# Sample rows of seven projection groups as plain fp32 matmuls in four column groups, with the weights' division moved ahead and five banks for the projections

## The chip, the cores and the metric

The kernel runs on 1 core of one Trainium2 chip. The metric is the device time of one execution in microseconds (us); less is better.

## What is computed

One inference step of a one-layer hybrid decoder. 1024 prompt rows (`SEQ`) and 8 sample rows (`DEC_BATCH`, one new token each) of width 1024 are normalised and go through one combined input projection, whose columns are split among an attention head group with three branches and a retention head group:

```python
parts = jnp.split(rms_norm(x, norm_g) @ w_in, SPLIT_POINTS, axis=-1)
q = rms_norm(parts[0].reshape(b, t, NSA_HEADS, HEAD_DIM), q_norm_g)
...
q_r = rotary(parts[9].reshape(b, t, RET_HEADS, RET_KDIM), pos)
k_r = rotary(parts[10].reshape(b, t, RET_HEADS, RET_KDIM), pos) * (RET_KDIM ** -0.5)
v_r = parts[11].reshape(b, t, RET_HEADS, RET_VDIM)
```

`project` is called for the prompt and for the sample with the same weights `w_in`. Behind it come compression of keys and values, attention, retention with a state, and one output projection with a residual.

## The kernel before, in words

The program is a row of stages, each with its own block of five engine programs and a barrier between them (`between`). The change lies in the first, `project` (line 186).

**Tiles and groups.** The 1032 rows are nine row tiles: eight of 128 prompt rows (`t` = 0 to 7) and the sample tile of 8 rows (`t` = `TT` = 8, `NT` = 9). The columns are eight groups in the order `qr, kr, vr, zr, q, wg, kv, zn`, all of 512 columns but `wg` (280). The loops run over groups outside and row tiles inside; `i = 9g + t`. The depth of 1024 is eight tiles of 128 (`KT`).

**Split precision.** Rows and weights are each held as a rounded high part and a low part that is the rest. On TensorE `proj` (line 806) makes three matmuls per depth tile (lines 818 to 820: high by high, low weights by high rows, high weights by low rows), 24 for a row tile, the sample tile included. ScalarE's `split_w` (line 435, activation at 441) rounds a depth tile of the next group's weights to `w_high`; VectorE's `split_w` (line 586, subtraction at 590) makes `w_low`. The text calls each of these instructions a half; there are eight on either engine per group. There is one buffer of each part, so ScalarE waits per depth tile for `w_used`, which TensorE raises during the sample tile, the last user of a group's weights. The raw weights come over SP's queue (`load_w`, line 262), for each depth tile once the low part of the group before is made.

**Banks.** Row tile `i` accumulates in PSUM bank `i % 3`; `bank_free` (line 232), raised by VectorE, tells TensorE that the tile that used the bank last is evacuated. Banks 3 and 4 take transposes, 5 to 7 the retention's scores and outputs.

**Evacuation.** `evac` on ScalarE (line 447) and VectorE (line 593) turns the sums into rotated rows (`qr`, `kr`; the last addition on GpSimd, line 399), gated rows (`zr`, `zn`), or normalised rows (`q`, `wg`, `kv`: a square on ScalarE, sum and mean on VectorE at lines 640 and 642, the root on GpSimd at 384, the product on VectorE). `post` on TensorE (line 880) turns normalised rows by transposes, and ScalarE and VectorE split them (lines 497 and 682). In TensorE's loop (line 945) the `post` of tile `i - 1` stands behind the projection of tile `i`, that of the sample tile too.

**Retention inside vr.** TensorE's `turn_ret` (line 832), `score`, `grow` and `out_ret` work on one chunk of 128 rows per row tile, between parts of the projection. The turn of the first chunk waits until GpSimd has added all rotated rows of `qr` and `kr`, the sample rows among them.

**Order.** Each engine's program is written out by hand and runs in order; semaphores tie them.

## Time and profile before

| | |
|---|---|
| median of 3 runs | 1019.42 us (1018.35 to 1020.18) |
| the profiled execution's own time | 1015.06 us |
| its span in the profile | 1013.4 us |
| granted TensorE clock, mean | 0.968 of 2.4 GHz |
| TensorE (PE) busy | 933.8 us, 92% |
| VectorE (DVE) busy | 501.9 us, 50% |
| ScalarE (ACT) busy | 309.7 us, 31% |
| GpSimd (POOL) busy | 189.4 us, 19% |
| projection stage on TensorE, first to last projection matmul | 17 to 497 us |

Rows of a timeline give the start and the length in us, then engine, line, operation and operands (output first), how many instructions were merged into the row, and in brackets the idle time before it with what ended it. A matmul's recorded length is modelled and overlaps the next one, so the pace is read from the starts. A plain fp32 matmul (no split) is recorded as two passes, that is two rows or a count of two.

### The profile page before, as it was taken

The numbers are of one execution on the slowest core, as the hardware profiler recorded it, in microseconds if no ns is written. First come the engines' busy times: TensorE is split into PE (matmuls) and PEld (weight loads), VectorE is DVE, ScalarE is ACT, GpSimd is POOL, SyncE is SP. The second block draws the span as 40 slices with busy tenths as digits, with TensorE's granted clock in tenths as the row PEclk, the third lists the DMA queues.
The fourth block names the chain that finished last, engine by engine and source line by source line (L and its number), as shares of the span: only waits on it lengthen the run. The fifth ranks groups of instructions, "written<-read, shape, count | busy, mean of one in ns | idle before, by whom it ended". The sixth has DMA issues, their size and how long they took to land. (4 is left out here: it accounts for less than half of the span.)

```text
span 1013.4 us, 15464 instructions
## 1 busy us (share of the span) xinstructions
PE 933.8 (92%) x5223; PEld 706.3 (70%) x5223; DVE 501.9 (50%) x1072; ACT 309.7 (31%) x692; POOL 189.4 (19%) x234
## 2 busy tenths in 40 slices
PE   5999999999999989999778898999999996789998
PEld 3676879997768787868568775566665654566785
DVE  4764244446144555450156356766675744464522
ACT  4311032223032324241010355645655642211100
POOL 1222213333002221100053102111011021452000
PEclk9999999999999999999989778999999997999999
DMA  7407520002520023113395410000000025778621
GB/s 256 143 6 177 138 84 1 2 1 73 213 94 6 1 83 104 53 38 107 91 205 144 115 31 22 22 21 22 1 22 22 1 81 187 204 218 276 200 85 46
DMA packets 91004, 91.11 MB, mean 90 GB/s; under 512 B 27629, under 2 KB 69661, under 8 KB 90565
## 3 DMA queue, kind: packets, MB, share of 16 engines
q1 hardware_dynamic: 70546, 71.66, 23.4%
q10 hardware_dynamic: 16700, 9.36, 3.5%
q0 software_dynamic: 3680, 9.10, 3.2%
q8 instruction: 42, 0.69, 0.3%
q14 instruction: 36, 0.29, 0.1%
HBM read 75.51 MB, written 23.49 MB: 98 GB/s over the span
## 5 line engine op out<-in xcount | busy, mean ns | idle before, releaser
L818 PE MATMUL ps<-w_high,x_high 128*128 128x512 f32 (+3 forms) x576 | 225.3, 391 | 4.6 <-DVE w_low L590 2.7
L820 PE MATMUL ps<-w_high,x_low 128*128 128x512 f32 (+3 forms) x576 | 220.6, 383 | 0.0
L819 PE MATMUL ps<-w_low,x_high 128*128 128x512 f32 (+3 forms) x576 | 220.3, 382 | 0.0
L818 PEld LDWEIGHTS ps<-w_high,x_high 128*128 128x128 f32 (+1 forms) x576 | 102.9, 179 | 37.2 <-issue 7.4
L820 PEld LDWEIGHTS ps<-w_high,x_low 128*128 128x128 f32 (+1 forms) x576 | 102.6, 178 | 28.0
L819 PEld LDWEIGHTS ps<-w_low,x_high 128*128 128x128 f32 (+1 forms) x576 | 102.9, 179 | 26.1
L1629 PE MATMUL ps<-k_high,q_stack 128*128 128x512 f32 (+3 forms) x192 | 77.9, 409 | 12.8 <-DVE a_stats L1514 12.5
L384 POOL TENSOR_TENSOR stats<-stats,small 128x8 f32<-128x8 f32 (+3 forms) x35 | 40.8, 1165 | 226.1 <-DVE stats L642 170.8
L1629 PEld LDWEIGHTS ps<-k_high,q_stack 128*128 128x128 f32 x192 | 38.8, 202 | 54.4 <-DVE a_stats L1514 28.6
L1671 PE MATMUL ps<-weights_turned,v_nat 128*64 128x512 f32 x264 | 72.5, 631 | 0.0
L1630 PE MATMUL ps<-k_low,q_stack 128*128 128x512 f32 (+3 forms) x192 | 67.0, 356 | 0.0
L2246 PE MATMUL ps<-w_out_high,y_high 128*128 128x512 f32 (+1 forms) x144 | 61.1, 424 | 4.1 <-DVE w_out_low L1982 3.5
L1180 DVE COPY kcs<-ps 128x512 f32<-128x512 f32 x28 | 30.3, 1084 | 69.2 <-PE ps L1240 69.1
L1423 POOL TENSOR_TENSOR y_tile<-y_tile,branch_out 128x512 f32<-128x512 f32 x15 | 19.2, 1277 | 224.4 <-DVEq L1572 224.4
L2248 PE MATMUL ps<-w_out_high,y_low 128*128 128x512 f32 (+1 forms) x144 | 57.4, 399 | 0.0
L2247 PE MATMUL ps<-w_out_low,y_high 128*128 128x512 f32 (+1 forms) x144 | 57.2, 398 | 0.0
L1514 DVE CUSTOM_DVE_ANT_1 window_logits<-ps,bias_full 128x640 f32<-128x640 f32 (+3 forms) x56 | 39.1, 708 | 34.0 <-PE ps L1630 33.7
L1542 DVE COPY weights_turned<-ps 128x512 f32<-128x512 f32 x66 | 45.5, 690 | 20.3 <-PE ps L1650 15.8
L1444 ACT ACTIVATE full_logits<-full_logits,a_stats 128x128 f32<-128x128 f32 (+7 forms) x64 | 49.3, 771 | 20.3 <-DVE a_stats L1514 20.0
L441 ACT ACTIVATE w_high<-w_raw 128x512 fp32r<-128x512 f32 (+1 forms) x64 | 36.5, 602 | 57.2 <-PE ps L820 55.6
L1514 DVE CUSTOM_DVE_ANT_1 full_logits<-ps,bias_full 128x256 f32<-128x256 f32 (+6 forms) x56 | 45.0, 821 | 17.8 <-PE ps L1630 16.5
L1453 ACT ACTIVATE weights_turned<-ps 128x512 f32<-128x512 f32 x66 | 39.0, 591 | 47.9 <-PE ps L1650 47.9
(311 smaller groups left out, 1526.6 us busy)
## 6 DMA issues: line engine op xcount, KB each, us to landing
w_raw<-in_w_in SPq DMA_DIRECT2D x48, 256.0 KB, 4.4
tmp_skew<-tmp_table SPq DMA_DIRECT2D x8, 576.0 KB
bias_full<-tmp_skew SPq DMA_DIRECT2D x8, 512.0 KB, 5.4
w_out_raw<-in_w_out SPq DMA_DIRECT2D x16, 256.0 KB, 5.0
y_rows_in<-tmp_y SPq DMA_DIRECT2D x8, 512.0 KB, 4.5
x_rows<-in_x_prompt SPq DMA_DIRECT2D x8, 512.0 KB, 5.6
out_y_prompt<-out_rows SPq DMA_DIRECT2D x8, 512.0 KB, 5.5
x_tile<-in_x_prompt SPq DMA_DIRECT2D x6, 512.0 KB, 3.8
```

What stands on the lines that cost most here:

```text
L818: nc.tensor.matmul(out, s.xh[:, k, rows], s.wh[:, k, 0:w], start=(k == 0), stop=False)
L819: nc.tensor.matmul(out, s.xh[:, k, rows], s.wl[:, k, 0:w], start=False, stop=False)
L820: ins = nc.tensor.matmul(out, s.xl[:, k, rows], s.wh[:, k, 0:w], start=False, stop=(k == KT - 1))
L1444: nc.scalar.activation(lg[:, h, 0:P * n], lg[:, h, 0:P * n], ACT.Exp, scale=-1.0, bias=st[:, S_MIN + H * j + h:S_MIN + H * j + h + 1], acc ...
L1514: nc.vector.tensor_tensor_reduce(out=columns(lg[:, h, 0:1]), in0=columns(pair[:, 0:1]), in1=view(full[:, TT - n, h, 0:1], [H * P, n], [1, ...
L1542: nc.vector.tensor_copy(pt[:, k % RP, 1, :], bank(k, 1)).then_inc(taken_v, 1)
L1629: nc.tensor.matmul(out, q(h), s.kh[:, j, h // G, k0 + c:k0 + c + w], start=True, stop=False)
L1630: last = nc.tensor.matmul(out, q(h), s.kl[:, j, h // G, k0 + c:k0 + c + w], start=False, stop=not (masked and c == 0))
L1671: last = nc.tensor.matmul(s.ps[at, 6, :], s.v[:, j, t + 1 - n + b, at], pt[:, k % RP, kv, :], start=(b == 0), stop=(b == n - 1))
L2246: nc.tensor.matmul(to, yh[:, t % 2, k, 0:n], wh[:, k, cols], start=(k == 0), stop=False)
L2247: nc.tensor.matmul(to, yh[:, t % 2, k, 0:n], wl[:, k, cols], start=False, stop=False)
L2248: last = nc.tensor.matmul(to, yl[:, t % 2, k, 0:n], wh[:, k, cols], start=False, stop=(k == KT - 1))
```

## The change

Group `qr` is computed as before, its sample tile included. In the other seven groups the sample tile's 24 split matmuls are replaced:

- The 8 sample rows are kept in plain fp32, turned so that depth lies on partitions (`x_sample_turned`, copied by VectorE from the banks of the transposes).
- `sample_rows(g)` multiplies them with the raw weights of group `g`: eight plain fp32 matmuls, four depth tiles into four column groups of bank 5 (partitions 0, 32, 64, 96), in two rounds. It stands one group ahead: behind tile 4 of group `g - 1`, behind tile 7 in `qr`, and at the end of `vr`.
- `keep_parts(g)` on ScalarE copies the bank, four partial sums of 8 rows, to SBUF. At the sample tile's place one plain fp32 matmul with `to_rows`, a matrix of ones and zeros, adds the four parts into an ordinary bank (the fold); evacuation then goes on as before.
- `w_used` is raised in tile 7 (`last_tile`). ScalarE's `split_w` for the next group stands ahead of tile 7's evacuation; VectorE's eight halves are spread: four ahead of tile 7's evacuation and four ahead of the sample tile's in `kr` and `zr`; in `q`, `wg` and `kv` two inside tile 6's evacuation (between mean and root), three ahead of and two inside tile 7's, one ahead of the sample tile's. In `qr` and `vr` all eight stand where they stood.
- The projections may use banks 6 and 7 too, in all groups but `qr`, `vr` and the first three tiles of `zr`: the bank used longest ago is taken.
- The `post` of a group's tile 7 and of its sample tile move on TensorE into the next group: behind its tile 0, and behind four depth tiles of its tile 1. In `vr`'s first tile the turn stands behind seven depth tiles in place of five.
- SP waits for the sample rows of group `g - 1` before it loads the weights of group `g`.

The core of the diff:

```diff
+    bank_of, uses = [], []
+    for i in range(n_idx):
+        allowed = (0, 1, 2) if i < NT or 2 * NT <= i < 3 * NT + 3 else (0, 1, 2, 6, 7)
+        last_use = {b: max((j for j, c in enumerate(bank_of) if c == b), default=-1) for b in allowed}
+        bank_of.append(min(allowed, key=lambda b: (last_use[b], b)))
...
             def load_w(g):
+                if g >= 2:
+                    sp.wait_ge(parted, g - 1)
...
+            def keep_parts(g):
+                w = GROUPS[g][2]
+                act.wait_ge(parted, g)
+                act.wait_ge(projected, g * NT)
...
+                nc.scalar.activation(fold(g)[:, 0:w], s.ps[:, PART_BANK, 0:w], ACT.Copy).then_inc(parts_kept, 1)
...
+                    beside = g > 0 and KIND[g] != "vr"
+                    if t == (TT - 1 if beside else TT) and g + 1 < NG:
+                        split_w(g + 1)
                     if t == TT and g + 1 < NG:
-                        split_w(g + 1)
+                        keep_parts(g + 1)
...
+                    if meanwhile:
+                        split_w(i // NT + 1, meanwhile)
                     dve.wait_ge(k_root, ni + 1)
...
+                    beside, chain = g > 0 and KIND[g] != "vr", KIND[g] in ("wg", "kv", "q")
+                    if t == TT - 1 and beside and g + 1 < NG:
+                        split_w(g + 1, range(2, 5) if chain else range(0, 4))
                     if t == TT and g + 1 < NG:
-                        split_w(g + 1)
+                        split_w(g + 1, range((7 if chain else 4) if beside else 0, KT))
...
+                    if chain and g + 1 < NG and t in (TT - 2, TT - 1):
+                        evac(i, range(0, 2) if t == TT - 2 else range(5, 7))
+                    else:
+                        evac(i)
...
+            def sample_rows(g):
+
+                w = GROUPS[g][2]
+                if g >= 2:
+                    pe.wait_ge(parts_kept, g - 1)
+                else:
+                    pe.wait_ge(part_set, 1)
+                for r in range(2):
+                    for c in range(4):
+                        k = 4 * r + c
+                        pe.wait_ge(w_in[k], 16 * (g + 1))
+                        last = nc.tensor.matmul(s.ps[32 * c:32 * c + B, PART_BANK, 0:w], s.xrow[:, k, :], s.wraw[:, k, 0:w],
+                                                start=(r == 0), stop=(r == 1))
+                last.then_inc(parted, 1)
...
+                if g and t == TT:
+                    pe.wait_ge(parts_kept, g)
+                    nc.tensor.matmul(out, s.to_rows[:], fold(g)[:, 0:w], start=True, stop=True).then_inc(projected, 1)
+                    return
...
-                    if t == TT and k < KT - 1:
+                    if t == last_tile and k < KT - 1:
                         ins.then_inc(w_used, 1)
...
-                        proj(i, range(0, 5))
+                        proj(i, range(0, 7))
                         turn_ret(t)
-                        proj(i, range(5, KT))
+                        proj(i, range(7, KT))
...
+                elif t == 1 and post_evac_kind(i - 2):
+                    proj(i, range(0, 4))
+                    post(i - 2)
+                    proj(i, range(4, KT))
                 else:
                     proj(i)
-                if i >= 1 and post_evac_kind(i - 1):
-                    post(i - 1)
+                if t == (TT if kind == "vr" else 7 if i < NT else 4) and i // NT + 1 < NG:
+                    sample_rows(i // NT + 1)
+                due_now = i - 2 if t == 0 else i - 1
+                if i >= 2 and t < TT and post_evac_kind(due_now):
+                    post(due_now)
```

How the order moves, at three places. First VectorE at the end of group `q`, from the product of tile 6 to that of the sample tile (`q_doubled` is the product, `q_stack` the low parts of the tile before, `w_low` the division for `wg`). Before:

```order
L649 TENSOR_TENSOR q_doubled<-ps,stats 128x1024
L707 SCALAR_TENSOR_TENSOR q_stack<-ps,gain,q_stack 64x4x128 x2
L640 TENSOR_REDUCE stats<-squares 128x8
L642 TENSOR_SCALAR stats<-stats 128x8
L649 TENSOR_TENSOR q_doubled<-ps,stats 128x1024
L707 SCALAR_TENSOR_TENSOR q_stack<-ps,gain,q_stack 64x4x128 x2
L590 TENSOR_TENSOR w_low<-w_raw,w_high 128x280 x8
L640 TENSOR_REDUCE stats<-squares 8x8
L642 TENSOR_SCALAR stats<-stats 8x8
L654 TENSOR_TENSOR q_doubled<-ps,stats 8x4x64 x2
```

Now, from the two halves ahead of that same product:

```order
L618 TENSOR_TENSOR w_low<-w_raw,w_high 128x280 x2
L679 TENSOR_TENSOR q_doubled<-ps,stats 128x1024
L737 SCALAR_TENSOR_TENSOR q_stack<-ps,gain,q_stack 64x4x128 x2
L618 TENSOR_TENSOR w_low<-w_raw,w_high 128x280 x3
L668 TENSOR_REDUCE stats<-squares 128x8
L670 TENSOR_SCALAR stats<-stats 128x8
L618 TENSOR_TENSOR w_low<-w_raw,w_high 128x280 x2
L679 TENSOR_TENSOR q_doubled<-ps,stats 128x1024
L737 SCALAR_TENSOR_TENSOR q_stack<-ps,gain,q_stack 64x4x128 x2
L618 TENSOR_TENSOR w_low<-w_raw,w_high 128x280
L668 TENSOR_REDUCE stats<-squares 8x8
L670 TENSOR_SCALAR stats<-stats 8x8
```

The one run of eight halves has become four pieces of two, three, two and one between the steps of tiles 6 and 7.

Second TensorE at the same end, from the `post` of tile 6 to that of the sample tile (`8x512` are the sample tile's matmuls, `128x280` those of `wg`). Before:

```order
L890 MATMUL ps<-ident,q_doubled 128x128 x8
L818 MATMUL ps<-w_high,x_high 8x512
L819 MATMUL ps<-w_low,x_high 8x512
...
L820 MATMUL ps<-w_high,x_low 8x512
L890 MATMUL ps<-ident,q_doubled 128x128 x8
L818 MATMUL ps<-w_high,x_high 128x280
...
L820 MATMUL ps<-w_high,x_low 128x280
L916 MATMUL ps<-ident,q_doubled 128x8 x4
```

Now:

```order
L962 MATMUL ps<-ident,q_doubled 128x128 x8
L879 MATMUL ps<-row_parts_late,to_rows 8x512
L887 MATMUL ps<-w_high,x_high 128x280
...
L889 MATMUL ps<-w_high,x_low 128x280
L962 MATMUL ps<-ident,q_doubled 128x128 x8
L887 MATMUL ps<-w_high,x_high 128x280
...
L889 MATMUL ps<-w_high,x_low 128x280
L988 MATMUL ps<-ident,q_doubled 128x8 x4
```

The 24 matmuls have become one, tile 7's turn has moved behind the first tile of `wg`, and the sample tile's turn from there into its second tile.

Third TensorE in the first tile of `vr`, from the turn of the first chunk to its scores (`kt_zeroed`). Before:

```order
L841 MATMUL ps<-ident,q_ret 128x128 x4
L841 MATMUL ps<-ident,k_ret 128x128 x4
L818 MATMUL ps<-w_high,x_high 128x512
L819 MATMUL ps<-w_low,x_high 128x512
...
L852 MATMUL ps<-qt,kt_zeroed 128x128 x8
```

Now:

```order
L910 MATMUL ps<-ident,q_ret 128x128 x4
L910 MATMUL ps<-ident,k_ret 128x128 x4
L887 MATMUL ps<-w_high,x_high 128x512
L888 MATMUL ps<-w_low,x_high 128x512
L889 MATMUL ps<-w_high,x_low 128x512
L924 MATMUL ps<-qt,kt_zeroed 128x128 x8
```

Between turn and scores stand now three projection matmuls where nine stood.

## Rows read from the trace of the kernel before

**Rows 1.** The page's busy time of TensorE, its share and instructions.

```profile
PE 933.8 (92%) x5223; PEld 706.3 (70%) x5223; DVE 501.9 (50%) x1072; ACT 309.7 (31%) x692; POOL 189.4 (19%) x234
```

**Rows 2.** Stretches: us; PE, PEld, DVE, ACT, POOL busy (count), clock, DMA, GB/s.

```profile
129.81:145.75 15.94, 15.03 (x81) 9.94 (x80) 10.58 (x17) 7.32 (x12) 3.60 (x3) 1.00 0.27 89
233.78:244.26 10.48, 10.18 (x65) 6.53 (x64) 9.23 (x14) 5.87 (x11) 4.65 (x3) 1.00 0.01 3
290.59:296.62 6.03, 5.73 (x26) 2.08 (x24) 4.92 (x8) 5.08 (x9) 0.00 (x0) 1.00 0.12 45
347.59:366.35 18.76, 15.07 (x89) 11.18 (x88) 10.85 (x25) 7.51 (x19) 3.96 (x3) 0.91 0.33 113
...
387.26:390.47 3.21, 3.21 (x27) 2.09 (x25) 1.76 (x7) 3.14 (x10) 0.70 (x1) 1.00 0.13 40
387.26:397.97 10.71, 9.68 (x55) 6.85 (x53) 7.92 (x20) 6.06 (x18) 1.38 (x2) 1.00 0.09 26
439.95:452.45 12.50, 12.20 (x59) 7.17 (x57) 9.18 (x24) 10.29 (x22) 1.39 (x2) 1.00 0.08 24
```

**Rows 3.** Waits of PE, 80 to 500 us: waited for, us, times, longest.

```profile
PE ps L916 <- DVE q_stack L707: 3.4, 1, 3.4
PE ps L818 <- DVEq L629: 1.5, 1, 1.5
PE ps L896 <- DVE k_low L698: 0.7, 1, 0.7
```

**Rows 4.** Timeline of PE around a 32-column fp32 matmul block, 903 us.

```profile
903.19 0.40 PE L2247 MATMUL ps<-w_out_low,y_high 128*128 128x512 f32 x1
903.42 0.40 PE L2248 MATMUL ps<-w_out_high,y_low 128*128 128x512 f32 x1
903.75 2.77 PE L2215 MATMUL ps<-keys_turned,q_by_row 128*32 128x512 f32 x12
906.45 0.50 PE L2246 MATMUL ps<-w_out_high,y_high 128*128 128x512 f32 x1
```

**Rows 5.** Timeline of PE, 8-column fp32 matmuls in four column groups, 974 us.

```profile
973.97 0.28 PE L2278 MATMUL ps<-values_in_raw,pt_selected 128*8 128x128 f32 x2
973.99 0.28 PE L2278 MATMUL ps<-values_in_state,pt_selected 128*8 128x128 f32 x2
...
976.60 0.40 PE L2280 MATMUL ps<-cv_sample,pt_compressed 128*8 128x128 f32 x8
```

**Rows 6.** Timeline of PE around one table matmul in group qr, 41 us.

```profile
40.53 1.04 PE L929 MATMUL ps<-ident,x_tile 128*128 128x128 f32 x8
41.50 1.02 PE L937 MATMUL ps<-one_hot,rel_bias_masked 33*8 33x512 f32 x2
42.45 0.50 PE L818 MATMUL ps<-w_high,x_high 128*128 128x512 f32 x1
```

**Rows 7.** Timeline of DVE at the end of group q.

```profile
343.72 1.23 DVE L649 TENSOR_TENSOR q_doubled<-ps,stats 128x1024 f32<-128x1024 f32 x1 [1.75 <-POOL stats L384]
345.19 1.43 DVE L707 SCALAR_TENSOR_TENSOR q_stack<-ps,gain,q_stack 64x512 fp32r<-64x512 f32 x2 [0.24 <-DVE q_doubled L649]
347.62 0.69 DVE L640 TENSOR_REDUCE stats<-squares 128x8 f32<-128x512 f32 x1 [1.00 <-ACT squares L492]
...
353.19 2.97 DVE L590 TENSOR_TENSOR w_low<-w_raw,w_high 128x280 fp32r<-128x280 f32 x8
```

**Rows 8.** Timelines of ACT and DVE: eight halves of 512 columns, for kv.

```profile
388.31 4.28 ACT L441 ACTIVATE w_high<-w_raw 128x512 fp32r<-128x512 f32 x8
...
390.50 4.90 DVE L590 TENSOR_TENSOR w_low<-w_raw,w_high 128x512 fp32r<-128x512 f32 x8
```

**Rows 9.** Timelines of POOL and ACT in the first tile of vr.

```profile
138.84 1.27 POOL L399 TENSOR_TENSOR k_ret<-rotated 8x512 f32<-8x512 f32 x1 [6.10 <-DVE rotated L605]
...
141.78 1.20 ACT L570 ACTIVATE kt_zeroed<-ps 64x512 f32<-64x512 f32 x2
```

**Rows 10.** DMA issues of the page: KB each, us to landing.

```profile
w_raw<-in_w_in SPq DMA_DIRECT2D x48, 256.0 KB, 4.4
```

More of the change, by code:

```diff
@@ L167, in layout @@
     s.stat = m.put("stats", [P, 64])
+    s.xrow = m.put("x_sample_turned", [P, KT, B])
+    s.to_rows = m.put("to_rows", [P, B])
     assert m.at <= SB_END, m.at
@@ L212, in project @@
     cen = m.put("centred", [P, 512])
+    folds = [m.put("row_parts_early", [P, 512]), Memory(nc, s.rq_region + 4 * H * T).put("row_parts_late", [P, 512])]
+    fold = lambda g: folds[g // 4]
+    PART_BANK = 5
     vr = Memory(nc, s.kct_region).put("v_ret", [P, 2, 512])
@@ L220, in project @@
     kind_of = lambda i: KIND[i // NT]
+    bank_of, uses = [], []
[3 more added lines that the diff above has]
+        bank_of.append(min(allowed, key=lambda b: (last_use[b], b)))
+        uses.append(bank_of[:-1].count(bank_of[-1]))
+    uses_up_to = lambda b, g: bank_of[0:NT * g].count(b)
     stored = [[0, 0]]
@@ L231, in project @@
         projected, rows_in, = sem("projected"), sem("ret_rows_out")
-        bank_free = [sem(f"bank_free{b}") for b in range(3)]
+        bank_free = {b: sem(f"bank_free{b}") for b in (0, 1, 2, 6, 7)}
+        part_set, parted, parts_kept, rows_turned = sem("row_part_bank_set"), sem("row_parts"), sem("row_parts_kept"), sem("x_rows_turned")
         st_stored = [sem(f"st_stored{b}") for b in range(2)]
@@ L448, in evac @@
                 kind, t = kind_of(i), i % NT
-                n, ps = rows_of(t), s.ps[0:rows_of(t), i % 3, :]
+                n, ps = rows_of(t), s.ps[0:rows_of(t), bank_of[i], :]
                 if kind == "vr":
@@ L530, in square @@
                                      accum_out=s.stat[0:n, t:t + 1]).then_inc(sum_ready, 1)
+            def keep_parts(g):
+                w = GROUPS[g][2]
+                act.wait_ge(parted, g)
+                act.wait_ge(projected, g * NT)
+                if g == 1:
+                    act.wait_ge(tab_stored, 16)
+                if g == 4:
+                    act.wait_ge(rows_in, 48)
+                nc.scalar.activation(fold(g)[:, 0:w], s.ps[:, PART_BANK, 0:w], ACT.Copy).then_inc(parts_kept, 1)
             def x_high(t):
@@ L591, in split_w, with evac @@
                                             ALU.subtract).then_inc(w_low, 1)
-            def evac(i):
+            def evac(i, meanwhile=None):
                 kind, t = kind_of(i), i % NT
-                n, ps = rows_of(t), s.ps[0:rows_of(t), i % 3, :]
-                free = bank_free[i % 3]
+                n, ps = rows_of(t), s.ps[0:rows_of(t), bank_of[i], :]
+                free = bank_free[bank_of[i]]
                 if kind in ("qr", "kr"):
@@ L732, in x_low @@
                                             ALU.subtract).then_inc(low_ready, 1)
+                    if t == TT:
+                        nc.vector.tensor_copy(s.xrow[:, 4 * half:4 * half + 4, :], view(s.ps[:, 3 + j % 3, 0:1], [P, 4], [1, n])).then_inc(rows_turned, 1)
+                if t == TT:
+                    dve.wait_ge(rows_turned, 3)
+                    nc.vector.memset(s.ps[:, PART_BANK, :], 0.0).then_inc(part_set, 1)
             def keep_table(j):
@@ L739, in _ @@
             nc.vector.memset(s.stat[:], 0.0).then_inc(stat_set, 1)
+            dve.wait_ge(ident_ready, 2)
+            nc.vector.tensor_reduce(s.to_rows[:], view(s.ident[:, 0:1], [1, B], [32, 4]), AX, ALU.add).then_inc(rows_turned, 1)
             dve.wait_ge(scale_in, 32)
@@ L797, in _ @@
                         retention_norm(nc, s, dve, own, cen, P, s.ps[:, 7, :], r_out, t, gn_done, t - 1, cen_ready, gn_sq, gn_mean)
-                    evac(i)
+                    if chain and g + 1 < NG and t in (TT - 2, TT - 1):
+                        evac(i, range(0, 2) if t == TT - 2 else range(5, 7))
+                    else:
+                        evac(i)
                     if i >= 1 and post_evac_kind(i - 1):
@@ L808, in proj @@
                 n, w = rows_of(t), GROUPS[g][2]
-                if i >= 3 and some[0] == 0:
-                    pe.wait_ge(bank_free[i % 3], (i - 3) // 3 + 1)
+                out = s.ps[0:n, bank_of[i], 0:w]
+                last_tile = TT if g == 0 else TT - 1
+                if some[0] == 0:
+                    if uses[i]:
+                        pe.wait_ge(bank_free[bank_of[i]], uses[i])
+                    if bank_of[i] >= 6 and g == 1:
+                        pe.wait_ge(tab_kept, N_HOT)
+                    if bank_of[i] >= 6 and kind_of(i) == "zr":
+                        pe.wait_ge(r_scd, 2 * TT)
+                        pe.wait_ge(cen_ready, TT)
+                if g and t == TT:
+                    pe.wait_ge(parts_kept, g)
+                    nc.tensor.matmul(out, s.to_rows[:], fold(g)[:, 0:w], start=True, stop=True).then_inc(projected, 1)
+                    return
                 if g == 0 and some[0] == 0:
@@ L816, in proj @@
                     rows = slice(P * t, P * t + n)
-                    out = s.ps[0:n, i % 3, 0:w]
                     nc.tensor.matmul(out, s.xh[:, k, rows], s.wh[:, k, 0:w], start=(k == 0), stop=False)
@@ L824, in proj @@
                     return
-                if t == TT:
+                if t == last_tile:
                     ins.then_inc(w_used, 1)
@@ L849, in score @@
                     pe.wait_ge(state_set, 4)
+                    pe.wait_ge(parts_kept, KIND.index("vr"))
+                    for b in (6, 7):
+                        pe.wait_ge(bank_free[b], uses_up_to(b, KIND.index("vr")))
                 for e in range(2):
```

## The prediction, made before the changed kernel ran

> **What bounds the kernel now.** I read the page's table of busy time first, then the stretches at the ends of the projection groups, then TensorE's waits, and last single rows of matmuls that resemble the new ones. TensorE is busy for 92% of the span [rows 1]; in the projection stage (17 to 497 us) it is the path, because the stretches at every group's end show it busy for nearly their whole length [rows 2]. So what the change takes off TensorE there comes off the time, unless a wait takes its place. The waits of that stage are few and short [rows 3], and each sits near a group's end, where the change works. The stages behind the projection begin after a barrier and keep their code; I take them as moved, not changed.
>
> The sum is made against the profiled execution, 1015.06 us (span 1013.4). The median of the runs shown is 1019.42, 0.43% above it; the gain in us is subtracted from the median.
>
> **Removed.** A split-precision matmul of 512 columns starts 0.23 us after the one before it, 903.19 to 903.42 [rows 4], so a tile of 24 takes 5.55 us, sample tile or not: at zr's end the sample tile and the drain behind it take 6.03 [rows 2], which leaves 0.48 for the drain (TensorE waits for its own last matmul through `w_used`). The drain stays; it only moves to the end of tile 7. In wg, with 280 columns, the tile takes 3.21 [rows 2]. Six times 5.55 and once 3.21 make **36.5 us removed**.
>
> **Added: the sample rows.** Eight plain fp32 matmuls, 8 columns of weights each, recorded as two passes apiece. Two kinds of rows show their price. The 32-column fp32 matmuls of L2215, 512 wide, go in pairs of two column groups: 12 records from 903.75 to 906.45 [rows 4], 0.45 us for each round of two records with the change back to full width in it, and an entry of 0.33 where 0.23 is usual, 0.10 more. The 8-column matmuls of L2278, 128 wide, go four at a time, in exactly the placement the change uses: 96 records in 24 rounds from 973.97 to 976.60, 0.11 us a round [rows 5], a quarter of the 512-wide round, as the widths are. Four rounds then cost 4 x 0.45 + 0.10 = 1.90 us at 512 columns and 1.1 at 280 (by the ratio of columns). No row shows four groups at 512 columns; the low bound is this, the high one is one group after another (a rival below). I take the low one: it is the nearest in both respects. 6 x 1.90 + 1.1 = **12.5 us added**. Their data wait for nothing: the weights of the next group land 4.4 us after their issue [rows 10], early in the group, and the sample rows come behind tile 4 (7 in the first group, the last place in vr).
>
> The row on the way back to full width bears on a rule of the Trainium skill. The matmul at 906.45 starts some 0.1 us later than a round would make it [rows 4]. The Trainium skill, TensorEngine Tiling (Array Packing), Key Properties, states that a change of tiling mode drains TensorE. Read strictly, as the whole modelled tail of a 0.40 us matmul behind its 0.23 pitch, each of the 14 excursions would cost about 0.15 us more, and the sum would be 2 us smaller; by the rows it is as above.
>
> **Added: the fold.** One plain fp32 matmul per group, 8 columns by 512. Its like is the table's matmul in the first group: from 41.50 to the next projection matmul at 42.45 is 0.95 us [rows 6]; with the entry of 0.10 it is 1.05, in wg 0.65. Six and one make **6.95 us added**. So TensorE's own work falls by 36.5 - 12.5 - 6.95 = 17.05 us.
>
> **The division loses its cover.** ScalarE's eight halves for 512 columns take 4.28 us and VectorE's 4.90 [rows 8]; before, they ran beside the sample tile. Now `w_used` counts tile 7, and the next group starts 0.48 + 1.05 us behind it. I followed each end:
> - *vr to zr* (10.48 [rows 2]): the division starts when tile 7 ends; fold, growth, output and sample rows take about 7.9 us, longer than the 4.9 of the division. No wait.
> - *zr to q*: half of VectorE's halves lie beside tile 7, the rest behind one evacuation; the fifth is due about 4.2 us behind tile 7 and ready at 3.4. No wait. Five banks also end the wait of 1.5 us for a bank here (L818 on the queue of L629 [rows 3]): ScalarE's results stand late, but five tiles can now wait for it. **-1.5.**
> - *kr to vr* (15.94): the sample row's sum on GpSimd starts 9.03 us behind tile 7 [rows 2, 9]; half of the 6 us of division leaves that path, so it ends near 9.03 - 3.0 + 1.27 = 7.3 us. TensorE, with seven depth tiles in place of five ahead of the turn, arrives at 6.35 and waits 1.0 us; ScalarE's three copies behind the turn end 2.9 us after its start (the last at 142.98, the turn right behind the sum's end at 140.11 [rows 9]), and only eight transposes (0.97 with what follows [rows 6]) and three matmuls lie there, so about 1.3 more. Before, that place lost 0.8. New stretch 12.85 against 15.94: 3.1 instead of the 4.5 of the tile less the fold. **+1.4.**
> - *q to wg* (18.76, clock 0.91 in it): VectorE sets the pace. From the end of tile 7's matmuls: ScalarE's square is late by 0.4 behind its halves, so the reduction starts at 1.3; reduce and scale 0.9, the root 1.75, the product 1.23 [rows 7] end at 5.1; the low parts of tile 6, 1.43 [rows 7], at 6.5; the last half (2.97 / 8 [rows 7]) at 6.9. TensorE wants it at 5.2: 1.7 of wait. Then the sample row's evacuation and tile 7's low parts end near 11.8, wanted at 9.9: 1.9. One more of 0.4. With 9.5 us of work that is 13.5 in place of 18.76, 5.2 gained against 4.5 counted. **-0.7**; L916's 3.4 [rows 3] comes back as two shorter waits.
> - *wg to kv* (10.71): the last half is ready 0.7 late, while L896's 0.7 [rows 3] goes with the later turn. **-0.2.**
> - *kv to zn* (12.50) and zn's end: the last half is ready 0.7 before it is wanted. Nothing.
>
> The halves put between mean and root on VectorE are covered by the root's 1.75 us there [rows 7]; without that cover they would cost the chains of q, wg and kv up to 0.75 each time. The copies of the parts on ScalarE (7 of 0.6), VectorE's copies and the clearing of the bank lie where these engines are idle; uncovered, they would be about 5 us. SP's new wait before a load is on sample rows of two groups earlier, long done; the stores queued behind it are not held.
>
> **Sum:** 17.05 + 1.5 - 1.4 + 0.7 + 0.2 = 18.05 us. 1019.42 - 18.05 = **1001.4 us**. The unknowns are the new waits (I count 7.0 us of them; between none, which adds 7, and twice as many, which takes 7) and the granted clock: the stretch q to wg ran at 0.91 [rows 2] because of one long wait, and two shorter ones may or may not lower it. With a few us for the clock of the stages behind, whose phase moves, the forecast's own range is 995 to 1009.
>
> **The rivals.**
> 1. *The four column groups overlap only in part.* For it: no row has four streams of 512 columns. Against: [rows 4, 5]. Two at a time doubles the rounds: 6 x 1.8 + 1.0 = 11.8 us back, 1013.2. The Trainium skill, TensorE: Matmul & The Clock Gate, Measured speedup vs the span model, gives three column tiles 2.38 times one, not three; by it a round would stretch by a quarter, 2.9 us back, 1004.3, though the 24 rounds of four in [rows 5] show no stretch. Chance 0.07, two thirds of it for that milder form.
> 2. *The groups run one after another.* This ends on the other side: sixteen passes of 0.43 where four were counted, 12 x 0.43 = 5.1 us more in six groups and 2.8 in wg: 33.5 back, **1035, slower**. It decides from the point where a round lasts 2.6 times its present length, since 11.2 us of rounds stand against 18. Against it: [rows 4, 5] show the opposite. Chance 0.03.
> 3. *Waits at the group ends take most of the gain.* VectorE's program is in strict order, and a half that waits for ScalarE holds the evacuation behind it; if the last half came 1.5 us later than I count at all seven ends, 10 us go back: 1011. For it: q, wg and kv are chains in which every link was within 0.4 us of TensorE. Chance 0.12.
> 4. *The waits I count do not come*, or the clock stays up through q to wg: 995. Chance 0.12.
> 5. *The time does not move*, because the later stages give it back (their page loads start earlier but land no earlier): 1019. Those loads are issued behind the barrier or paced by the tiles, so against. Chance 0.02.
>
> **Numbers.** The forecast itself has 0.64. A measurement of this kernel tells about 0.2% (2 us) from no change. Faster by more than that: all of forecast, 1, 3 and 4, 0.95; the same 0.02; slower 0.03. The range 994 to 1011 leaves out rivals 2 and 5, the two-at-a-time form of 1, and the far ends of 3 and 4: some 2 in 10 at most.
>
> **What would show it.** In the profile after: rows of the sample matmuls in rounds of four with starts about a hundredth of a us apart and 0.43 us between rounds, about 1.9 us from the first to the next full-width matmul; one fold of 1.05; next groups' first tiles with waits of about 1.7 on the divided weights in wg, 0.7 in kv, none in zr, q and zn; no bank wait in zr; the projection's last matmul at about 479 instead of 497. The forecast is wrong if the rounds are longer than 0.5 us, if the first tiles of zr, q or zn wait, or if the stages behind the barrier change length by more than 5 us.

## The result, and the profile after

The changed kernel takes **999.76 us**, the median of 4 runs (999.06 to 1000.96), beside 1018.88 for the kernel before in the same job (1016.44 to 1020.18): a ratio of 0.9823 with a 95% interval of [0.9807, 0.9839]. Forecast were 1001.4 us in a range of 994 to 1011, and 18.05 us of gain; the medians show 19.1.

The two profiled executions show less: 1000.10 us after (span 998.4) against 1015.06 before (span 1013.4), 15.0 us. The execution of before was the fastest of that kernel on record. That gap is taken up with the last experiment.

The page's busy time, answering to [rows 1]: TensorE lost 12.4 us of busy time, less than the 17 of the sum. The busy time is no exact account, since recorded lengths are modelled, so the sum is better compared with starts, further down.

```profile
PE 921.4 (92%) x5181; PEld 697.6 (70%) x5181; DVE 503.9 (50%) x1076; ACT 313.5 (31%) x699; POOL 190.2 (19%) x234
```

TensorE's timeline around one group of sample rows (in `kr`, for `vr`) and one fold with the next group's first matmul; they answer to [rows 4 to 6].

```profile
115.51 0.40 PE L889 MATMUL ps<-w_high,x_low 128*128 128x512 f32 x1
115.84 1.90 PE L860 MATMUL ps<-w_raw,x_sample_turned 128*8 128x512 f32 x16
117.67 0.50 PE L887 MATMUL ps<-w_high,x_high 128*128 128x512 f32 x1
118.01 0.39 PE L888 MATMUL ps<-w_low,x_high 128*128 128x512 f32 x1
...
134.95 1.02 PE L879 MATMUL ps<-row_parts_early,to_rows 128*8 128x512 f32 x2 [0.30 <-PE ps L889]
135.90 0.50 PE L887 MATMUL ps<-w_high,x_high 128*128 128x512 f32 x1
```

Sixteen passes go in 1.83 us from the first to the next full-width matmul. In the single records the four of a round start 6 to 8 ns apart and the rounds 0.43 us apart. With the late entry (0.33 where 0.23 is usual) that is 1.93 us; the forecast had 1.90. Behind the block the second full-width matmul also starts late, 0.34 us after the first. The fold takes 0.95 us. Its entry lies in the drain of tile 7, which stands there anyway (0.30 us of idle time ahead of the fold in `kr`, 0.41 in `zr`), so it costs 0.95 to 1.05 for the 1.05 forecast.

TensorE's waits from 60 to 480 us, answering to [rows 3] (waited for, us in total, times, longest):

```profile
PE ps L887 <- DVE w_low L618: 2.3, 2, 2.0
PE ps L988 <- DVE q_stack L737: 2.0, 1, 2.0
PE ps L910 <- POOL k_ret L414: 1.5, 1, 1.5
PE ps L962 <- DVE k_low L728: 1.2, 2, 1.1
PE ps L924 <- ACT kt_zeroed L598: 1.1, 1, 1.1
```

The first two are the two waits of `q` to `wg`, the third and fifth those of the turn and of the scores in `vr`, the fourth one at the end of `wg`. None stands in `zr`, `q` or `zn`, and the bank wait of `zr` is gone.

Stretches of the changed kernel at the groups' ends, from the fold on, answering to [rows 2] (columns as there):

```profile
134.95:148.06 13.11, 10.57 (x58) 7.96 (x59) 8.00 (x13) 3.28 (x6) 3.60 (x3) 1.00 0.33 104
236.56:243.95 7.39, 7.39 (x58) 4.97 (x59) 6.59 (x11) 5.21 (x10) 4.23 (x3) 1.00 0.01 2
291.14:292.09 0.95, 0.95 (x2) 0.09 (x2) 0.11 (x1) 0.81 (x2) 0.00 (x0) 1.00 0.00 0
344.80:356.00 11.20, 7.22 (x50) 5.94 (x50) 7.64 (x16) 3.66 (x10) 3.39 (x2) 0.99 0.43 139
356.00:358.00 2.00, 2.00 (x10) 1.98 (x10) 1.15 (x5) 0.56 (x2) 0.70 (x1) 0.50 0.00 0
383.39:389.78 6.39, 6.39 (x29) 4.80 (x29) 5.28 (x16) 2.25 (x11) 1.76 (x2) 1.00 0.12 35
435.23:442.20 6.97, 6.97 (x31) 5.01 (x31) 5.46 (x17) 2.46 (x10) 1.76 (x2) 1.00 0.14 40
```

The row from 356 to 358 is the one that was not forecast: behind the two waits of `q` to `wg` the granted clock stood at 0.50, TensorE's lower level of 1.2 GHz.

Read from the starts of the same row tiles in both traces, the time goes as follows (us; a gain is positive; `kr` 7 is tile 7 of `kr`):

| place | forecast | profile pair |
|---|---|---|
| first group, up to `qr` 1 | 0 | -0.7 |
| sample rows, six places (the seventh is in vr to zr) | -10.6 | -10.7 |
| kr to vr (`kr` 7 to `vr` 1) | 3.1 | 2.4 |
| vr to zr, its sample rows included | 2.6 | 2.6 |
| bank wait in zr | 1.5 | 1.6 |
| zr to q | 4.5 | 4.5 |
| q to wg (`q` 7 to `wg` 2) | 5.2 | 3.5 |
| wg to kv | 2.75 | 2.15 |
| kv to zn | 4.5 | 4.4 |
| zn to the next stage | 4.5 | 4.3 |
| sum at the next stage's first matmul | 18.05 | 14.1 |
| behind the projection | 0 | 0.9 |

### The profile page after: what moved, and what is told of

It reads as the page before. It is cut to its first block and busy times, and to the rows that moved or that the text cites. A ratio compares the mean times of both kernels' runs of the same rounds, so it can differ in the third digit from the quotient of the medians.

```text
span 998.4 us, 15424 instructions
## 1 busy us (share of the span) xinstructions
PE 921.4 (92%) x5181; PEld 697.6 (70%) x5181; DVE 503.9 (50%) x1076; ACT 313.5 (31%) x699; POOL 190.2 (19%) x234
## 5 line engine op out<-in xcount | busy, mean ns | idle before, releaser
L887 PE MATMUL ps<-w_high,x_high 128*128 128x512 f32 (+1 forms) x520 | 204.8, 394 | 4.4 <-DVE w_low L618 4.4
L889 PE MATMUL ps<-w_high,x_low 128*128 128x512 f32 (+1 forms) x520 | 199.8, 384 | 0.0
L888 PE MATMUL ps<-w_low,x_high 128*128 128x512 f32 (+1 forms) x520 | 199.4, 383 | 0.0
L887 PEld LDWEIGHTS ps<-w_high,x_high 128*128 128x128 f32 x520 | 98.0, 188 | 36.3 <-issue 12.9
L889 PEld LDWEIGHTS ps<-w_high,x_low 128*128 128x128 f32 x520 | 97.8, 188 | 21.0
L888 PEld LDWEIGHTS ps<-w_low,x_high 128*128 128x128 f32 x520 | 98.2, 189 | 19.0
```

Of the source, the lines that this page charges most:

```text
L887: nc.tensor.matmul(out, s.xh[:, k, rows], s.wh[:, k, 0:w], start=(k == 0), stop=False)
L888: nc.tensor.matmul(out, s.xh[:, k, rows], s.wl[:, k, 0:w], start=False, stop=False)
L889: ins = nc.tensor.matmul(out, s.xl[:, k, rows], s.wh[:, k, 0:w], start=False, stop=(k == KT - 1))
```

## The experiments

Theory: the gain is the sample tile's work less the sample rows and folds, and it reaches the time only because the new order brings the division and the posts in time. Rivals: the gain is the new order's alone, or TensorE's work counts whatever the order.

**1. One column group.** All eight sample matmuls in partitions 0 to 7, one behind the other.

```diff
-                        last = nc.tensor.matmul(s.ps[32 * c:32 * c + B, PART_BANK, 0:w], s.xrow[:, k, :], s.wraw[:, k, 0:w],
-                                                start=(r == 0), stop=(r == 1))
+                        last = nc.tensor.matmul(s.ps[0:B, PART_BANK, 0:w], s.xrow[:, k, :], s.wraw[:, k, 0:w],
+                                                start=(k == 0), stop=(k == KT - 1))
...
-            nc.vector.tensor_reduce(s.to_rows[:], view(s.ident[:, 0:1], [1, B], [32, 4]), AX, ALU.add).then_inc(rows_turned, 1)
+            nc.vector.tensor_reduce(s.to_rows[:], view(s.ident[:, 0:1], [1, B], [32, 1]), AX, ALU.add).then_inc(rows_turned, 1)
```

> The changed kernel with the eight sample matmuls of a group all in the first column group, one after the other, and a fold that adds that one part. Theory (the sample rows are cheap because four column groups run at once): sixteen passes of 0.43 us per group of 512 where four rounds of 0.43 stood, 12 x 0.43 = 5.1 us more in six groups and about 2.8 in wg, 33.5 us in all: about 1033 us, slower than the kernel before. Rival (the gain comes from the new order at the group ends, banks and posts, and the placement in column groups matters little): within 5 us of the changed kernel, 1000 to 1005.

Measured: 1035.64 us, ratio 1.0166 [1.0135, 1.0197]. The same sample rows in its timeline of TensorE (the end of the block is the next tile):

```profile
120.71 3.60 PE L860 MATMUL ps<-w_raw,x_sample_turned 128*8 128x512 f32 x8
...
127.68 0.50 PE L887 MATMUL ps<-w_high,x_high 128*128 128x512 f32 x1
```

From the first pass to the next tile it is 6.97 us where 1.83 stood: 5.14 more, and twelve passes 0.429 us apart make 5.15. The projection's last matmul starts 33.3 us later. So the column groups do run at once, fully, and the four of them decide whether this change gains or loses: the second rival of the prediction (1035, slower) is this kernel, to a us.

**2. Either half alone.** `rows_only` keeps sample rows and folds and takes everything else back; `schedule_only` keeps banks, posts and the later turn, with the old sample tile and the old division.

```diff
# rows_only, against the changed kernel
-        allowed = (0, 1, 2) if i < NT or 2 * NT <= i < 3 * NT + 3 else (0, 1, 2, 6, 7)
+        allowed = (0, 1, 2)
-                    if t == (TT - 1 if beside else TT) and g + 1 < NG:
+                    if t == TT and g + 1 < NG:
                         split_w(g + 1)
...
-                        split_w(g + 1, range((7 if chain else 4) if beside else 0, KT))
+                        split_w(g + 1)
...
+                if i >= 1 and post_evac_kind(i - 1):
+                    post(i - 1)
...
# schedule_only, which leaves out the early division and the sample rows too
-                last_tile = TT if g == 0 else TT - 1
+                last_tile = TT
...
-                if g and t == TT:
-                    pe.wait_ge(parts_kept, g)
-                    nc.tensor.matmul(out, s.to_rows[:], fold(g)[:, 0:w], start=True, stop=True).then_inc(projected, 1)
-                    return
...
```

> Sample rows and fold as in the changed kernel, but everything around them as before: three banks, all of the division ahead of the sample tile's evacuation on ScalarE and VectorE, the posts behind the next tile, the turn behind five depth tiles. Theory (TensorE's saved work of 17 us is worth only what the division's cover allows): kr to vr gives back about 4, wg to kv and kv to zn about 2 each, zr to q some 0.3 and the bank wait stays, so 8 to 10 us of gain, 1009 to 1012 us. Rival (the new order is of no weight, TensorE's work alone sets the time): 1001 to 1003.

> The other half: five banks, the posts moved into the next group and the turn behind seven depth tiles, but the sample tile as 24 split matmuls and the division where it stood before (it cannot start earlier while the sample tile is the last reader). Theory: the bank wait of zr (1.5 us) goes, TensorE's wait at the end of q (3.4) shortens by 2 to 3, that of wg by 0.5: 3 to 5 us of gain, 1014 to 1016. Rival (VectorE sets the pace at those ends whatever TensorE's order): only the 1.5 of the bank, 1017 to 1018.

Measured: `rows_only` 1018.23 us, 0.9992 [0.9976, 1.0009]; `schedule_only` 1013.79 us, 0.9951 [0.9925, 0.9976]. Of the first, theory and rival both expected too much: the 17 us saved on TensorE bring nothing that can be measured. Its waits, from 60 to 480 us, are where they went:

```profile
PE ps L882 <- DVE w_low L618: 4.4, 3, 2.2
PE ps L955 <- DVE q_stack L737: 4.1, 1, 4.1
PE ps L905 <- POOL k_ret L414: 3.0, 1, 3.0
PE ps L981 <- DVE q_stack L737: 2.3, 1, 2.3
PE ps L965 <- DVE k_low L728: 2.3, 1, 2.3
PE ps L955 <- DVE k_low L728: 2.3, 1, 2.3
```

These rows hold 18.4 us of waits, where the kernel before has 5.6 in [rows 3] and 0.6 ahead of the turn. The sample tile's time has become waiting for what used to run beside it, and behind three of the waits the clock is lower (0.57 from 357 to 361 us, 0.65 from 395 to 404, 0.79 from 452 to 460). In the execution that was profiled the clock also fell in the first group (0.57 from 36 to 40 us), which costs it 2.2 us against the changed kernel; whether the other executions have that is not shown. The other half gives 5.5 us (1019.33 in this job), a little over what was expected; by the starts of its tiles 1.7 us are the bank's and 2.2 come at `q` to `wg`, where L916's wait halved. Apart the halves make 6.6 us, together 19. But the two are not the whole change: the early, spread division is in neither, since it cannot start before the sample tile has let go of the weights. What it adds is tried next.

**3. One part of the order taken back at a time,** the rest as changed: VectorE's eight halves in one place again (`no_spread`), the posts where they were (`posts_back`), three banks (`three_banks`).

```diff
# no_spread
-                    if t == TT - 1 and beside and g + 1 < NG:
-                        split_w(g + 1, range(2, 5) if chain else range(0, 4))
                     if t == TT and g + 1 < NG:
-                        split_w(g + 1, range((7 if chain else 4) if beside else 0, KT))
+                        split_w(g + 1)
...
-                        evac(i, range(0, 2) if t == TT - 2 else range(5, 7))
# posts_back
-                due_now = i - 2 if t == 0 else i - 1
-                if i >= 2 and t < TT and post_evac_kind(due_now):
-                    post(due_now)
+                if i >= 1 and post_evac_kind(i - 1):
+                    post(i - 1)
# three_banks
-        allowed = (0, 1, 2) if i < NT or 2 * NT <= i < 3 * NT + 3 else (0, 1, 2, 6, 7)
+        allowed = (0, 1, 2)
...
```

> The changed kernel with VectorE's eight halves all in one place, ahead of the sample tile's evacuation, as before; ScalarE's stay ahead of tile 7's evacuation. Theory (the place of the halves in VectorE's program is what keeps the heads of the groups free): kr to vr +2.9, zr to q +1.7, q to wg +0.6, wg to kv and kv to zn +0.8 each: 1005 to 1009 us, and the first tile of q waits for its divided weights. Rival (the posts and the banks carry it, the halves would be in time anyway): 999 to 1002.

> The changed kernel with the posts of tile 7 and of the sample tile back where they were, behind the sample tile's fold and behind the next group's tile 0. Theory (the post of tile 7 needs the whole chain square, sum, root, product, and nothing lies between but a fold of 1 us): waits of about 3 ahead of it in q, wg and kv; q to wg loses 1.6 of it, since the last half and the second post then wait less, wg to kv 3.4, kv to zn 3: 1006 to 1010 us. Rival (VectorE sets the pace there, the wait only moves): 1000 to 1002.

> The changed kernel with its projections back in three banks, everything else as changed. Theory (the banks are worth the one wait of 1.5 us in zr): 1001 to 1002 us, with a wait of 0.7 to 1.5 ahead of zr's tile 6 and nowhere else. Rival (five banks also let TensorE run ahead of the evacuation at the ends of q, wg and kv): 1003 or more, with bank waits in those groups.

Measured: `no_spread` 1021.48 us, 1.0013 [0.9988, 1.0038]; `posts_back` 1014.39, 0.9931 [0.9899, 0.9962]; `three_banks` 1001.13, 0.9809 [0.978, 0.9839].

*The spread* is worth about 20 us (1.0013 against 0.9823): taken back alone, it takes all of the gain with it. Theory and rival both had this far too small. `no_spread` is also the two halves of experiment 2 put together, with ScalarE's early halves but without VectorE's spread, and it is slower than `schedule_only` (0.9951): without the spread, taking 17 us of matmuls off TensorE makes this kernel slower. VectorE's timeline of `no_spread` at the end of `q` shows why:

```profile
352.21 0.69 DVE L668 TENSOR_REDUCE stats<-squares 128x8 f32<-128x512 f32 x1 [1.44 <-ACT squares L507]
352.93 0.17 DVE L670 TENSOR_SCALAR stats<-stats 128x8 f32<-128x8 f32 x1
354.85 1.23 DVE L679 TENSOR_TENSOR q_doubled<-ps,stats 128x1024 f32<-128x1024 f32 x1 [1.75 <-POOL stats L399]
356.31 1.43 DVE L737 SCALAR_TENSOR_TENSOR q_stack<-ps,gain,q_stack 64x512 fp32r<-64x512 f32 x2 [0.24 <-DVE q_doubled L679]
357.77 2.97 DVE L618 TENSOR_TENSOR w_low<-w_raw,w_high 128x280 fp32r<-128x280 f32 x8
```

At the sample tile's place the halves stand behind tile 7's whole chain (sum, root, product) and tile 6's low parts, 5.6 us after the sum starts, and they are short themselves. In the changed kernel seven of the eight are done by then, in the 1.75 us idle before the product and ahead of the sum. The expectation priced the halves' own length and forgot the chain ahead of them. TensorE finds nothing to do at the heads of `vr`, `q`, `wg`, `kv` and `zn` (waits for `w_low` of 2.2, 2.3, 4.9, 4.3 and 3.4 us; with 0.3 in `kr` they make 17.4, against 2.3 in the changed kernel), and behind each of these five it runs slower. TensorE's stretches of `no_spread` from the end of those waits to the next tile (in `vr` to the wait for the scores); the column behind POOL's is the clock:

```profile
138.40:147.50 9.10, 9.10 (x32) 7.29 (x32) 5.30 (x10) 0.29 (x1) 2.31 (x2) 0.66 0.11 29
298.00:305.30 7.30, 7.22 (x25) 5.76 (x26) 4.73 (x8) 0.00 (x0) 0.00 (x0) 0.77 0.23 69
358.30:364.50 6.20, 6.13 (x33) 6.16 (x34) 3.94 (x11) 0.24 (x1) 1.62 (x1) 0.62 0.85 278
397.50:404.70 7.20, 7.17 (x27) 5.76 (x27) 4.90 (x11) 0.00 (x0) 0.69 (x1) 0.79 0.05 13
454.50:462.20 7.70, 7.65 (x29) 6.14 (x30) 4.94 (x12) 0.00 (x0) 0.69 (x1) 0.78 0.07 18
```

The first tile of `q` takes 7.2 us there instead of 5.7, those of `kv` and `zn` 1.3 and 1.6 more than in the changed kernel. These three waits, of 2.3, 4.3 and 3.4 us, thus cost 1.3 to 1.6 us each on top of themselves.

*The posts.* `posts_back` waits 4.5, 4.1 and 3.4 us ahead of tile 7's posts, each longer than the 3 expected, because a post also needs the low parts of the tile before it, which stand behind tile 7's product on VectorE. Behind each the clock is low again (0.69, 0.77 and 0.79 up to the next tile); in the first tiles of `kv` and `zn` that costs 1.6 us. At `q` to `wg` it only replaces the two waits of the changed kernel (0.9 us lost); `wg` to `kv` and `kv` to `zn` lose 5.3 and 5.0. Another 2.3 us of this profile come from its first group, where the clock fell as in `rows_only` (0.57 from 36 to 40 us). The posts are worth about 11 us (0.9931 against 0.9823), in the expectation's direction and over its upper end of 1010. Single executions range from 1007.59 to 1016.12, so how much of the 11 is the posts' and how much the first group's clock is open; the trace shows 11.2 at the three ends.

*The banks.* The wait in `zr` is back, 1.3 us ahead of tile 6, and no bank wait elsewhere. The median is 1.4 us above the changed kernel's, which these runs cannot tell from nothing; the trace holds the place and the size.

**4. A version with three ends rearranged** (`better`), and one of the three alone (`better_vr`).

```diff
# both: VectorE, end of kr; TensorE, vr's first tile
...
+                        if KIND[g] == "kr" and t == TT:
+                            split_w(g + 1, range(6, KT))
...
-                        proj(i, range(0, 7))
+                        proj(i, range(0, 6))
                         turn_ret(t)
# better alone: VectorE, q's tile 7 and wg's tiles 6 and 7; TensorE, posts of q half a tile and a tile later
...
-                        evac(i, range(0, 2) if t == TT - 2 else range(5, 7))
+                        evac(i, (None if KIND[g] == "wg" else range(0, 2)) if t == TT - 2 else range(5, 7 if KIND[g] == "kv" else KT))
...
-                elif t == 1 and post_evac_kind(i - 2):
+                elif kind == "wg" and t in (1, 2, 3) or t == 1 and post_evac_kind(i - 2):
                     proj(i, range(0, 4))
-                    post(i - 2)
+                    post(i - 3 if kind == "wg" and t < 3 else i - 2)
...
```

> The changed kernel with three ends rearranged. kr to vr: VectorE's last two halves behind the sample tile's evacuation, the turn behind six depth tiles. q to wg: the last half inside tile 7's evacuation, the posts of q's tile 7 and sample tile half a tile and a tile later. wg to kv: no halves inside tile 6's evacuation, three inside tile 7's. Theory (the waits there of 1.5 + 1.1, 2.0 + 2.0 with the fallen clock behind them, and 1.1 us come from the place of single instructions): kr to vr 1.7 less, q to wg 3.4 less and 1 less by the clock, wg to kv 0.8 less, 992 to 995 us. Rival (VectorE's chain as a whole sets these ends, so the waits only move on): 998 to 1000.

> Of the version above only the end kr to vr: VectorE's last two halves behind the sample tile's evacuation and the turn behind six depth tiles, all else as in the changed kernel. Theory (the turn waits for GpSimd's sum of the sample row, which stands behind VectorE's halves): the 1.2 us that the profile of the version above shows at this place, so 998.5 us, with a wait of 0.9 to 1.0 ahead of the turn and none ahead of the scores. Rival (a gain there is given back in vr, whose tiles wait for each other): 999.5 to 1000.5, the first tile of zr starting when it did.

Measured: `better` **996.73 us**, 0.9781 [0.9759, 0.9802], the fastest of all; `better_vr` 999.38, 0.9814 [0.9788, 0.984], which the medians cannot tell from the changed kernel. By the starts of the tiles, `better` gains 1.2 us at `kr` to `vr`, 2.0 at `q` to `wg` and 0.8 at `wg` to `kv`; `better_vr` gains 1.2 at the first and keeps it to the end of `zn`, so in the trace its theory held. The turn's wait fell to 0.95 and the scores' is gone. At `q` to `wg` both were half right: the two waits of 2.0 and the slow clock went (the stretches from 340 to 370 us all have 1.00), and `wg`'s tile 2 starts 6.4 us earlier than in the changed kernel, counted from `q`'s end, but by tile 4 only 2.0 of it is left. `better`'s timeline of TensorE, its waits alone:

```profile
354.57 0.38 PE L991 MATMUL ps<-ident,q_doubled 8*128 8x8 f32 x4 [0.77 <-DVE q_stack L737]
357.27 0.41 PE L965 MATMUL ps<-ident,squares 128*128 128x128 f32 x2 [0.58 <-DVEq L740]
360.49 0.41 PE L965 MATMUL ps<-ident,squares 128*128 128x128 f32 x2 [1.27 <-DVE k_low L728]
363.36 0.41 PE L965 MATMUL ps<-ident,squares 128*128 128x128 f32 x2 [0.91 <-DVE k_low L728]
```

VectorE's chain sets the pace of `wg`'s first tiles too, so a wait that was taken away at the head comes back, smaller, at the posts.

**5. Both kernels again,** for second profiles.

> The kernel before, once more, for its profile: the one on record took 1015.06 us where the median is 1019, so the pair of profiles shows 15.0 us of gain where the medians show 19.1. Theory (that execution began with a faster start of the first projection tiles, which every changed kernel here reaches 0.7 to 1.3 us later, and had a higher clock behind the projection): a span of 1016 to 1019, the first group about 1 us later, the rest of the difference behind the projection. Rival (the projection stage itself varies between executions by some us): the groups after the first differ by more than 1 us as well.

> The changed kernel once more, beside the kernel before on the same chip, for a second profile and a direct comparison with the version above. Theory (the waits sit where the program puts them, the clock moves a little): 999 to 1001 us, the same waits of about 1.5 and 1.1 in vr's first tile, 2.0 and 2.0 in wg, 1.1 at wg's end, within 0.1 us each; the first tiles and the tile behind wg's second wait vary by up to 1.6 us with the clock. Rival (the waits are chance too): they differ by more than 0.3 us.

Measured: `before_again` 1019.79 us (ratio 0.9996 [0.9975, 1.0017]), span 1018.9; `after_again` 999.88 against 1018.30 in its job (0.9821 [0.9789, 0.9854]), span 997.4. This pair of profiles shows 21.5 us, the first 15.0, so the medians' 19.1 and 18.4 lie between. Half of the 5.5 us that the second execution of before took longer lies in the projection: 0.3 in the first group, 1.1 in the bank wait of `zr`, 1.2 behind L916's wait, where the clock stayed low for longer. The other 2.75 us lie behind it, where the twelve kept profiles take between 511.2 us (`after_again`) and 515.0 (`before_again`) from the first matmul of the next stage to the end; this stretch varies by itself. Rows of `before_again`: the bank wait, and the stretches around L916.

```profile
280.75 0.49 PE L818 MATMUL ps<-w_high,x_high 128*128 128x512 f32 x1 [2.59 <-DVEq L629]
```

```profile
361.00:364.00 3.00, 1.38 (x8) 1.38 (x9) 2.07 (x5) 0.56 (x2) 0.70 (x1) 0.64 0.46 176
364.00:367.00 3.00, 3.00 (x14) 3.00 (x14) 0.80 (x4) 0.00 (x0) 0.00 (x0) 0.50 0.00 0
367.00:371.00 4.00, 4.00 (x27) 4.00 (x27) 0.85 (x4) 0.97 (x5) 0.70 (x1) 0.79 0.01 2
```

So the theory held for the stage behind and the rival for the projection, where a wait's length and the clock behind it differ between executions. In `after_again` four of the five waits repeat to within 0.04 us (1.45, 1.07, 2.02, 1.05). The second one of `wg` is 0.76 instead of 1.96: there the clock fell earlier, in the tile between the two waits, and TensorE arrived later at the second.

## Why the prediction was right

- **What bounds it.** Right: what left TensorE in the projection left the time. But experiments 2 and 3 show how narrow that was: with the halves in one place nothing is left. And "busy for nearly their whole length" does not hold for `q` to `wg`, 15.07 of 18.76 us [rows 2], which is where the sum was furthest off.
- **Removed, sample rows, folds.** Right to 0.1 us each, but for the rows computed in `wg`, which are 0.2 us cheaper; the rounds at 0.43, the entry as in [rows 4]. The serial kernel shows the price of the rival. Of the drain that the Trainium skill, TensorEngine Tiling (Array Packing), Key Properties, states for a change of mode, the records show 0.10 us on the way in (0.33 where 0.23 is usual) and 0.20 on the way out (0.52 where a round is 0.43, then 0.34 where 0.23 is usual). The stretch that rival 1 took from the Trainium skill, TensorE: Matmul & The Clock Gate, Measured speedup vs the span model (2.38 for three tiles), does not show: four groups keep the round at 0.43.
- **vr to zr, zr to q, kv to zn, zn's end.** Right, no waits, within 0.2 us.
- **The bank of zr.** Right for the execution that was read; a second one had 2.6 us there, and the five banks take whatever it is.
- **kr to vr: the step that failed** is "half of the 6 us of division leaves that path". Eight halves do not cost the same. Rows of VectorE and GpSimd in the changed kernel:

```profile
136.28 3.59 DVE L618 TENSOR_TENSOR w_low<-w_raw,w_high 128x512 fp32r<-128x512 f32 x4
139.79 0.67 DVE L629 TENSOR_TENSOR rotated<-ps,rope 8x512 f32<-8x512 f32 x1
...
136.21 1.30 POOL L414 TENSOR_TENSOR k_ret<-rotated 128x512 f32<-128x512 f32 x1 [4.35 <-DVE rotated L633]
141.20 1.25 POOL L414 TENSOR_TENSOR k_ret<-rotated 8x512 f32<-8x512 f32 x1 [3.69 <-DVE rotated L633]
```

  Four halves take 3.5 us, not 3.0: in the single records the first lasts 1.78 and the others start 0.60 apart. GpSimd adds tile 7's rows from 136.21 to 137.51, just during that first one. Halving the count left the slow one in. So GpSimd's sum of the sample row ends 8.0 us behind tile 7 (at 142.45), where 7.3 was forecast. By the starts on TensorE, the turn comes 1.86 us behind the matmul ahead of it and the scores 1.48, where 0.23 is usual: 1.6 and 1.25 us lost for the 1.0 and 1.3 forecast, 0.6 of the 0.7 us of gain that are missing.
- **q to wg: the term was mis-sized.** The waits were forecast at 1.7 and 1.9 and measured at 2.0 and 2.0, and the mechanism (VectorE's order of tile 7's product, tile 6's low parts, last half) was right; what was left out of the sum is the clock behind them, 0.50 from 356 to 358 us. Twelve matmuls start 0.23 us apart there where 0.13 is usual, about 1.3 us in all. The prediction named it as an unknown and put nothing in for it. The small third wait (0.4 forecast) did not come, because the slow matmuls fill its place. In `three_banks` and `after_again`, where they ran at full clock, it is there with 0.57 us; the row of `three_banks`:

```profile
360.53 0.41 PE L960 MATMUL ps<-ident,squares 128*128 128x128 f32 x2 [0.57 <-DVEq L740]
```

  By both, `wg` 2 then starts 0.7 us earlier: so much, and not 1.3, is what the clock takes at this place.
- **wg to kv: the wrong wait.** The last half was in time; instead the post of tile 6 waited 1.1 us. VectorE's row of the two halves between mean and product:

```profile
380.04 1.30 DVE L618 TENSOR_TENSOR w_low<-w_raw,w_high 128x512 fp32r<-128x512 f32 x2 [0.86 <-ACT w_high L456]
381.25 0.28 DVE L698 SCALAR_TENSOR_TENSOR stage<-ps,stats,k_gain 128x64 f32<-128x64 f32 x1
```

  They wait 0.86 us for ScalarE's halves and take 1.2, while the root that was to cover them takes 0.70 here, for two heads, not the 1.75 of `q` [rows 7]. The cover was taken from the wrong group. Without them (`better`) the 0.8 us came back.
- **The first group.** 0.7 us lost that nothing in the sum stood for. In the first tile of `qr` nine matmuls run at the slower pace of 0.43 us before it turns to 0.23; in the execution of before it is six, in its repeat seven. All changed kernels here start `qr` 1 between 0.2 and 1.5 us later than the two executions of before; whether the change or chance sets it was not tried.
- **The median.** The sum of 18.05 us came out between the two pairs of profiles. In the pair that it was worked out from it is 4 us too large: the last split matmul starts at 481.4 us and the last fold at 482.2, for about 479 forecast. Its errors (1.7 + 0.7 + 0.6 + 0.7 too much) were met by what the profile of before held too little of: a shorter bank wait, a shorter slow clock, a faster stage behind. That the median came out 1.6 us from the forecast is to that extent luck.

## What to carry to other kernels

Ahead of removing work from the bounding engine, list what ran beside that work: here 17 us of saved matmuls were worth nothing until VectorE's instructions had been put into places where it waited anyway. Price a wait with the clock that may fall behind it, and read the cover of a moved instruction from the row of its own group. Profile the kernel before twice when the forecast is a sum of single waits.

## What the runs showed of the hardware

Four column groups of 8 columns by 512 plain fp32 overlap without a loss: 1.83 us for sixteen passes, 6.97 us when they go through one. VectorE's subtraction of 128 x 512 is followed by the next one 0.60 us later when it runs alone, and 1.70 us later when an addition of GpSimd on 512 columns runs beside it. In four traces (`before`, `after`, `better_vr`, `no_spread`) such a subtraction lasts 1.5 to 1.8 us beside one of GpSimd's wide retention operations and 0.7 in every other place, beside GpSimd's small roots too. Behind the 2.0 us wait at the head of `wg` the granted clock fell at once in some executions (0.53 from 353 to 356 us in `three_banks`, 0.58 in `after_again`) and only behind the second wait in others (0.50 from 356 to 358 in the changed kernel's first profile). Where it fell early, TensorE came later to the second wait and that one shrank from 1.96 to 0.3 and 0.76: the slow clock lay in time that would have been waited, and `wg`'s tile 2 then started 0.7 us earlier. Nor does every such wait lower the clock: behind waits of 2.2 and 1.9 us at the heads of `vr` and `q` in `rows_only` the stretches have 1.00.
